# A norm after a matmul stage: the last block's squares summed by TensorE directly, its weight split and its products moved behind them

## The chip, the cores and the metric

The kernel runs on one core of one Trainium2 chip. The metric is the device time of one launch in microseconds (us). Engines are named as in the profile: PE is TensorE, DVE is VectorE, ACT is ScalarE, POOL is GpSimd, SP is SyncE (here it only issues weight loads).

## The reference

One sequence of 512 tokens with 1024 features goes through a conditioned block (gated mixer and convolution mixer, `w_out`, feed-forward of 2816), a final modulated norm, and then a second network: attention with two kinds of heads, a feed-forward, a pooling mixer and another feed-forward. What matters here is that each stage which ends in a product with a weight matrix is followed by a norm over the 1024 features of every token:

```python
def rmsnorm(x, g):
    xf = x.astype(jnp.float32)
    y = xf * lax.rsqrt(jnp.mean(xf * xf, axis=-1, keepdims=True) + EPS)
    return (y * g.astype(jnp.float32)).astype(x.dtype)
...
        x = x + gate1[:, None, :] * (y @ w_out[i])
        h2 = modulate(rmsnorm(x, norm2_g[i]), shift2, scale2)
```

In the first network the norm is taken of the renewed `x`. In the second it is taken of the stage's output `m`: `x` becomes `x + rmsnorm(m)`, and the norm of the new `x`, which opens the next stage, is derived from the sums of m*m, x*m and (gained m) squared.

## The kernel before

Features lie on the 128 partitions (8 chunks, `C`), tokens along the free axis (512). A weight matrix is read in blocks that give 128 output features: a block of 8 (or 11 for the down projections) tiles of 128x128. Each weight is split in a high and a low part so that three fast matmuls give fp32 accuracy: SP loads the raw block (`RAW`, 4 buffers), ACT rounds it to `WH` (L263, `split_hi`), DVE subtracts to get `WL` (L267, `split_lo`), 2 buffers each. PE computes a block with 3 matmuls per tile (L319 to L321) into one of two PSUM banks, and signals `mm`. ACT and DVE work in a written order of their own, one step per block: the split of the block two further on, and then the evacuation of the block that was just finished. `phase_splits` writes that order; at the last block of a stage the split step belongs to the second block of the next stage.

Six norms follow such a stage: `n2` after `w_out`, `nf` after `ffo0`, `r1` after `att_out`, `r2` after `ffo1`, `r3` after the pooling stage and `r4` after `ffo2`. The norm of each needs the sum of squares over all features of a token:

- In `n2` and `nf` DVE adds the gated bank to `X` (`dve_gated`, L513), ACT squares the chunk of `X` into `TMP` (`act_gated`, L522), DVE adds `TMP` to the running sum `ACC` (L518).
- In `r1`, `r2`, `r4` ACT (`act_m`) copies the bank to `M` with a gain (L528), squares it into `TMP` (L532 or L535) and, in `r1` and `r2`, squares the gained bank into `TMM` (L536); then DVE (`dve_m`) adds `TMP` to `ACC` (L555), multiplies `M` by `X` into `TXM` (L544) and adds `TMM` to `SMM` and `TXM` to `SXM` (`dve_cross`, L547 and L550). The pooling stage does the same in `pool_squares` (L1565, L1570, L1573) and `pool_sums` (L1965 to L1971).
- Then the chain of the norm: PE sums `ACC` over the partitions with four 1-column matmuls (`pe_sum`, L384, 8 records), DVE scales the mean (L408), POOL takes the power of -1/2 (L438), DVE lays it on a diagonal (L417), PE spreads it over all partitions (`pe_bcast`, L389, 2 records), and DVE starts on the normed chunks (L492, L586 or L569).

In `r1`, `r2`, `r3` PE sums `SXM` and `SMM` after the broadcast (`pe_sum_cross`). During `w_out` DVE also adds blocks of the conditioning matrix (`ada_step`, L1627), as many behind each block as `ADA_STEPS` says. In `r3` the splits of the first two blocks of `ffi2` run on DVE under the power and under the broadcast (`dve_renew`, `under_power` and `under_broadcast`).

Of the kernel before, what the change touches and what calls it, by code (L numbers as in the profile page):

```python
# [38 lines left out]
ADA_STEPS = [2, 2, 1, 1, 1, 1, 1, 1, 2, 2, 2, 2, 2, 0, 0, 0] + [2, 2, 2, 2, 1, 1, 1, 1]  # L39
# [34 lines left out]
def build_program(nc, xT, vec, ada_w, w_in, w_out, ffi, ffo, ln_rows, ws, bs, att_w, att_out, bf, pe, w1, w2,  # L74
                  pool_w, f2i, f2o, outT):
    ctx = ExitStack()
    with ctx:
# [160 lines left out]
        class Norm:  # L238

            def __init__(self, count, turn, at, n_acc_):  # L240
# [47 lines left out]
        def phase_splits(name, eng, step, evac):  # L288

            kc, nxt = kc_of(name), follow(name)  # L290
            uniform = nxt is not None and nxt[0] == kc
# [217 lines left out]
        def dve_gated(nj_, name, m, b, gate0):  # L509
# [5 lines left out]
                                           ALU.mult, ALU.add).then_inc(ev[b], 1)  # L515
            nc.vector.wait_ge(n_sq, nj_.sq + m[0] + 1)
# [410 lines left out]
        def _(pe_):  # L927
# [155 lines left out]
            pe_sum(nj["n2"])  # L1083
# [6 lines left out]
            pe_sum(nj["nf"])  # L1090
# [188 lines left out]
            pe_sum(nj["r1"])  # L1279
# [4 lines left out]
            pe_sum(nj["r2"])  # L1284
# [34 lines left out]
            pe_sum(nj["r3"])  # L1319
# [4 lines left out]
            pe_sum(nj["r4"])  # L1324
# [4 lines left out]
        def _(act):  # L1329
# [73 lines left out]
            def last_square(k):  # L1403
                if k == 1:
# [6 lines left out]
                         lambda g, t: act_gated(nj["n2"], "w_out", 4 * g + t, t % 2, 2 * g + t // 2))  # L1411
# [3 lines left out]
                         lambda g, t: act_gated(nj["nf"], "ffo0", 2 * g + t // 2, t // 2, g) if t % 2 else None)  # L1415
# [113 lines left out]
            def m_phase(name, r, norm_col, js=None):  # L1529
# [4 lines left out]
                else:  # L1534
                    phase_splits(name, act, act_step, lambda g, t: act_m(
                        nj[r], name, 4 * g + t, t % 2, N0[name] + 4 * g + t + 1,
                        VEC[:, bass.ds(COL["norm_g2"] + norm_col + 4 * g + t, 1)], js))
# [23 lines left out]
            def pool_squares(o):  # L1561
# [3 lines left out]
                act.activation(M[:, o, :], PS[b][:, :], ACT.Copy, scale=PG[:, o:o + 1])  # L1565
# [4 lines left out]
                act.activation(ACC if o == 0 else TMP[:, b, :], PS[b][:, :], ACT.Square, scale=vcol("pool_s", o))  # L1570
# [16 lines left out]
        def _(dve):  # L1587
# [471 lines left out]
```

## Time and profile before

| | us |
|---|---|
| median of 3 runs | 1854.68 (1853.14 to 1855.72) |
| the profiled execution | 1853.88 |
| its span, first to last instruction | 1852.1 |
| PE busy in the span | 1714.6 (93%) |
| DVE busy | 900.6 (49%) |
| ACT busy | 662.0 (36%) |
| POOL busy | 189.6 (10%) |

The profiled execution took 1.8 us more than its span, and 0.8 us less than the median. PE is busy for nearly all of the span, but "busy" holds time at the lower clock and time between a weight stage and the next. The page gives the mean granted TensorE clock as 0.959 of full speed.

### The profile page before, as it was taken

The page shows a single profiled execution, that of the slowest core. Times are in us where ns is not written, and L with a number is a line of the kernel's source. Part 1 is how long each engine was busy: PE and PEld are TensorE (multiplying, and loading weights), DVE is VectorE, ACT ScalarE, POOL GpSimd, SP SyncE. Part 2 cuts the span into 40 slices and gives each one's busy share as a digit, 9 for nine tenths or more (in the row PEclk, how much of TensorE's full clock was granted, in tenths as well). Part 3 has the DMA queues.
Part 4 walks back from the last instruction along what each step waited for, and adds up shares of the span by engine and source line. Part 5 has one row for each costly group of instructions (what it writes and reads, how often), then busy time and mean ns, then how long its engine had stood idle before and what let it go on. Part 6 is the DMA issues. An engine that isn't in the chain of part 4 may idle for free.

```text
span 1852.1 us, 21986 instructions
## 1 busy us (share of the span) xinstructions
PE 1714.6 (93%) x8095; PEld 1336.5 (72%) x8095; DVE 900.6 (49%) x1340; ACT 662.0 (36%) x949; POOL 189.6 (10%) x186
## 2 busy tenths in 40 slices
PE   2999889999999859999999899999998799999996
PEld 1657668888888637766667688888887588888884
DVE  6865674533322262355656644444334844444223
ACT  1324334444312241455555344443224433333221
POOL 4001119910000060000000000001100000000000
PEclk9999889999999969999999799999998799999998
DMA  8564144522322231111102122223221022223221
GB/s 284 197 204 146 65 163 170 181 91 102 108 94 93 68 62 66 58 46 35 35 24 69 47 101 92 100 91 117 93 76 54 32 99 97 96 96 114 93 77 46
DMA packets 49111, 179.73 MB, mean 97 GB/s; under 512 B 5984, under 2 KB 6656, under 8 KB 48928
## 3 DMA queue, kind: packets, MB, share of 16 engines
q1 hardware_dynamic: 44896, 166.75, 26.2%
q0 software_dynamic: 3008, 10.59, 2.1%
q10 hardware_dynamic: 1152, 1.66, 0.3%
q8 instruction: 34, 0.56, 0.1%
q14 instruction: 21, 0.17, 0.0%
HBM read 173.56 MB, written 2.10 MB: 95 GB/s over the span
## 4 chain that ended last, share of the span: by engine, by line
PE 66%; issue 22%; DVE 8%; ACT 2%; POOL 1%; DMA 1%; ACTq 1%; POOLq 0%; DVEq 0%; SPq 0%
PE bank L319 15%; PE bank L321 15%; PE bank L320 15%; PE bank L1138 3%; PE bank L1140 2%; PE bank L1139 2%; PE bank L1198 2%; PE bank L1242 2%; PE bank L1218 2%; DVE ada_acc L1598 1%; PE bank L389 1%; PE bank L1296 1%; PE bank L1123 1%; DVE tmp L492 1%; DMA raw<-in_ada_w 1%
## 5 line engine op out<-in xcount | busy, mean ns | idle before, releaser
L267 DVE TENSOR_TENSOR w_lo<-raw,w_hi 128x1024 fp32r<-128x1024 f32 (+1 forms) x236 | 319.1, 1352 | 684.9 <-ACT w_hi L263 684.8
L319 PE MATMUL bank<-h_hi,w_hi 128*128 128x512 f32 x1248 | 495.0, 397 | 6.9 <-DVE h_lo L485 3.5
L320 PE MATMUL bank<-h_lo,w_hi 128*128 128x512 f32 x1248 | 488.2, 391 | 0.0
L321 PE MATMUL bank<-h_hi,w_lo 128*128 128x512 f32 x1248 | 488.1, 391 | 0.0
L263 ACT ACTIVATE w_hi<-raw 128x1024 fp32r<-128x1024 f32 (+1 forms) x236 | 265.6, 1126 | 584.6 <-PE bank L321 516.0
L319 PEld LDWEIGHTS bank<-h_hi,w_hi 128*128 128x128 f32 x1248 | 235.6, 189 | 70.0 <-issue 11.0
L321 PEld LDWEIGHTS bank<-h_hi,w_lo 128*128 128x128 f32 x1248 | 235.7, 189 | 49.6
L320 PEld LDWEIGHTS bank<-h_lo,w_hi 128*128 128x128 f32 x1248 | 235.9, 189 | 48.2 <-issue 1.0
L319 PE MATMUL bank<-hid_hi,w_hi 128*128 128x512 f32 x528 | 209.4, 397 | 0.0
L321 PE MATMUL bank<-hid_hi,w_lo 128*128 128x512 f32 x528 | 209.2, 396 | 0.0
L320 PE MATMUL bank<-hid_lo,w_hi 128*128 128x512 f32 x528 | 209.1, 396 | 0.0
L438 POOL TENSOR_TENSOR stat<-stat,nhalf 128x4 f32<-128x4 f32 x10 | 11.1, 1111 | 1195.7 <-DVE stat L408 1195.7
L320 PEld LDWEIGHTS bank<-hid_lo,w_hi 128*128 128x128 f32 x528 | 99.4, 188 | 24.3
L321 PEld LDWEIGHTS bank<-hid_hi,w_lo 128*128 128x128 f32 x528 | 99.3, 188 | 24.4
L319 PEld LDWEIGHTS bank<-hid_hi,w_hi 128*128 128x128 f32 x528 | 99.3, 188 | 24.2
L384 PE MATMUL bank<-ones,tmp 128*128 128x1 f32 x80 | 15.9, 319 | 66.0 <-POOL tmp L464 43.8
L636 ACT ACTIVATE hid_hi<-tmp 128x512 f32 (+1 forms) x44 | 27.9, 635 | 119.8 <-DVE tmp L652 119.8
L384 PEld LDWEIGHTS bank<-ones,tmp 128*128 128x128 f32 x80 | 15.6, 286 | 70.2 <-issue 30.5
L1480 ACT ACTIVATE p_t<-bank 128x1024 f32<-128x1024 f32 (+4 forms) x52 | 37.9, 729 | 78.5 <-PE bank L1218 70.8
L1138 PE MATMUL bank<-h_hi,w_hi 128*128 128x512 f32 x128 | 59.1, 461 | 0.0
L1497 ACT ACTIVATE scores<-scores,att_stat 128x512 f32<-128x512 f32 (+3 forms) x96 | 52.8, 552 | 9.0 <-DVE att_stat L1873 8.9
L633 ACT ACTIVATE tmp<-tmp 128x512 f32<-128x512 f32 x44 | 27.8, 633 | 71.1 <-DVE tmp L645 71.1
(310 smaller groups left out, 1969.4 us busy)
## 6 DMA issues: line engine op xcount, KB each, us to landing
raw<-in_f2i SPq DMA_DIRECT2D x88, 512.0 KB, 3.2
raw<-in_ffi SPq DMA_DIRECT2D x44, 512.0 KB, 3.2
raw<-in_f2o SPq DMA_DIRECT2D x32, 704.0 KB, 4.0
ada_w<-in_ada_w SPq DMA_DIRECT2D x32, 512.0 KB, 4.1
raw<-in_att_w SPq DMA_DIRECT2D x24, 512.0 KB, 3.2
raw<-in_ffo SPq DMA_DIRECT2D x16, 704.0 KB, 4.0
raw<-in_ada_w SPq DMA_DIRECT2D x16, 512.0 KB, 4.7
raw<-in_w_in SPq DMA_DIRECT2D x16, 512.0 KB, 5.2
```

Of the source, the lines that this page charges most:

```text
L263: nc.scalar.activation(WH[par][:, 0:kc * P], RAW[s][:, 0:kc * P], ACT.Copy).then_inc(whi, 1)
L267: nc.vector.tensor_tensor(WL[par][:, 0:kc * P], RAW[s][:, 0:kc * P], WH[par][:, 0:kc * P].bitcast(F32), ALU.subtract).then_inc(wlo, 1)
L319: pe_.matmul(bank[:, :], w_h, hi[:, k0 + k, :], start=start and k == 0, stop=False)
L320: pe_.matmul(bank[:, :], w_h, lo[:, k0 + k, :], start=False, stop=False)
L321: last = pe_.matmul(bank[:, :], w_l, hi[:, k0 + k, :], start=False, stop=stop and k == kc - 1)
L1138: pe_.matmul(PS[t][:, :], w_h, hi[:, k, :], start=first, stop=False)
L1139: pe_.matmul(PS[t][:, :], w_h, lo[:, k, :], start=False, stop=False)
L1140: m = pe_.matmul(PS[t][:, :], w_l, hi[:, k, :], start=False, stop=last)
L1198: m = pe_.matmul(QB[:, half, 0:L], lhs, rhs, start=kind != "fox", stop=True)
L1218: m = pe_.transpose(TB[:, half, j * P:(j + 1) * P], sc[:, j * P:(j + 1) * P], IDN[:, :])
L1480: act.activation(dst[:, :, 0:L], TB[0:rows, :, 0:L], ACT.Copy).then_inc(a6["pt"], 1)
L1497: act.activation(sc, sc, ACT.Exp, scale=-1.0, bias=AST[:, 0, col:col + 1], accum_out=AST[:, 1, col:col + 1]).then_inc(a6["ex"], 1)
```

## The change

In all six norms the last block (chunk 7) is treated apart.

- ACT squares the bank first and signals `n_sq`; the copy to `M` and the gained square come behind. This new order holds for every block of `r1` to `r4`.
- DVE no longer adds the last chunk's squares to `ACC`. PE sums seven chunks from `ACC` and then the eighth from `TMP` (`pe_sum_last`: four matmuls, a wait on `n_sq`, four matmuls, accumulating in the same four columns).
- The split of the next stage's second block is held back: on ACT behind the last square, on DVE behind the diagonal (`n2`, `nf`, `r1`).
- In `r1`, `r2`, `r3` the last product is under the power and the last two sums are under the broadcast. The `ffi2` splits that were there go behind `r2`'s renewal, ahead of the pooling sums.
- In `w_out` the last ada step moves from behind block 7 to behind block 4, and the mean is issued ahead of the two small conditioning operations.

The diff, cut to its core:

```diff
-ADA_STEPS = [...] + [2, 2, 2, 2, 1, 1, 1, 1]
+ADA_STEPS = [...] + [2, 2, 2, 2, 2, 1, 1, 0]
...
+        def last_split(name, step):
+            kc, rnd = follow(name)
+            step(N0[name] + 4 * G[name] + 1, 1, 1, kc, rnd)
...
-                    elif nxt is not None:
+                    elif nxt is not None and not (hold and t == 3):
                         step(n + 2, t % 2, t - 2, nxt[0], nxt[1])
...
+        def pe_sum_last(nj_):
+            nc.tensor.wait_ge(n_acc, nj_.acc_end)
+            for i in range(TC):
+                nc.tensor.matmul(NS[:, i:i + 1], ACC[:, i * P:(i + 1) * P], ONE[:, 0:1], start=i == 0, stop=False,
+                                 skip_group_check=True)
+            nc.tensor.wait_ge(n_sq, nj_.sq + C)
+            for i in range(TC):
+                m = nc.tensor.matmul(NS[:, i:i + 1], TMP[:, 1, i * P:(i + 1) * P], ONE[:, 0:1], start=False,
+                                     stop=i == TC - 1, skip_group_check=True)
+            m.then_inc(n_used, 1)
...
         def act_m(nj_, name, m, b, done, gain, js):
             nc.scalar.wait_ge(mm, done)
-            nc.scalar.activation(M[:, bass.ds(m, 1), :], PS[b][:, :].rearrange("p (a s) -> p a s", a=1), ACT.Copy,
-                                 scale=gain)
             nc.scalar.wait_ge(n_acc, nj_.acc + m)
+            if js is not None:
+                nc.scalar.wait_ge(n_mms, 9 * js + m + 1)
+            nc.scalar.activation(TMP[:, b, :], PS[b][:, :], ACT.Square).then_inc(n_sq, 1)
+            into = nc.scalar.activation(M[:, bass.ds(m, 1), :], PS[b][:, :].rearrange("p (a s) -> p a s", a=1),
+                                        ACT.Copy, scale=gain)
             if js is None:
-                nc.scalar.activation(TMP[:, b, :], PS[b][:, :], ACT.Square).then_inc(ev[b], 1)
+                into.then_inc(ev[b], 1)
             else:
-                nc.scalar.wait_ge(n_mms, 9 * js + m + 1)
-                nc.scalar.activation(TMP[:, b, :], PS[b][:, :], ACT.Square)
                 nc.scalar.activation(TMM[:, b, :], PS[b][:, :], ACT.Square, scale=gain).then_inc(ev[b], 1)
...
         def dve_m(nj_, name, m, b, half, js):
-            nc.vector.wait_ge(ev[b], O0[name] // 2 + half + 1)
+            nc.vector.wait_ge(n_sq, nj_.sq + m + 1)
             nc.vector.wait_ge(n_acc, nj_.acc + m + 1)
             nc.vector.tensor_tensor(ACC, ACC, TMP[:, b, :], ALU.add).then_inc(n_acc, 1)
             if js is not None:
+                nc.vector.wait_ge(ev[b], O0[name] // 2 + half + 1)
+                dve_product(m, b)
                 dve_cross(m, b, js)
...
+            dve_mean(nj["n2"], D)
             dve.wait_ge(ada_sum, 5)
             dve.tensor_tensor(MOD[:, 24:40], PS[5][:, 24:40], VEC[...], ALU.add).then_inc(mod_ready, 1)
-            dve_mean(nj["n2"], D)
             dve.wait_ge(mod_ready, 6)
             gain(1, 32, "norm2").then_inc(mod_ready, 1)
             dve_diag(nj["n2"], D, mean=False)
+            last_split("w_out", dve_step)
...
             dve_diag(nj["nf"], D)
+            last_split("ffo0", dve_step)
...
-            dve_renew(nj["r1"], nj["q1"], 0, xs[1], g1_, dve_low(nj["q1"], xs[1], g1_))
+            def last_cross():
+                dve_cross(C - 1, 1, 0)
+                last_split("att_out", dve_step)
+            dve_renew(nj["r1"], nj["q1"], 0, xs[1], g1_, dve_low(nj["q1"], xs[1], g1_),
+                      under_power=lambda: last_product("att_out"), under_broadcast=last_cross)
...
-            dve_renew(nj["r2"], nj["q2"], 1, xs[2], None, None, spread=False)
+            dve_renew(nj["r2"], nj["q2"], 1, xs[2], None, None, spread=False,
+                      under_power=lambda: last_product("ffo1"), under_broadcast=lambda: dve_cross(C - 1, 1, 1))
+            split_lo(N0["ffi2"], 0, 0, C)
+            split_lo(N0["ffi2"] + 1, 1, 1, C)
...
-            for o in range(C):
+            for o in range(C - 1):
                 pool_sums(o)
...
-                      under_power=lambda: split_lo(N0["ffi2"], 0, 0, C),
-                      under_broadcast=lambda: split_lo(N0["ffi2"] + 1, 1, 1, C))
+                      under_power=lambda: pool_product(C - 1, 1), under_broadcast=lambda: pool_cross(C - 1, 1))
```

Where `pe_sum` stood for `n2`, `nf` and `r1` to `r4`, `pe_sum_last` stands now.

## Rows read from the trace of the kernel before

**Rows 1.** Page, part 4: the chain that ended last, shares by engine.

```profile
PE 66%; issue 22%; DVE 8%; ACT 2%; POOL 1%; DMA 1%; ACTq 1%; POOLq 0%; DVEq 0%; SPq 0%
```

**Rows 2.** Timeline about `n2`: start us, us, engine, line, op, out<-in [idle before <-releaser].

```profile
254.25 0.39 PE L321 MATMUL bank<-h_hi,w_lo 128*128 128x512 f32 x1
254.68 1.06 ACT L263 ACTIVATE w_hi<-raw 128x1024 fp32r<-128x1024 f32 x1 [3.32 <-PE bank L321]
255.76 1.23 DVE L267 TENSOR_TENSOR w_lo<-raw,w_hi 128x1024 fp32r<-128x1024 f32 x1 [2.49 <-ACT w_hi L263]
256.91 0.74 DVE L513 SCALAR_TENSOR_TENSOR x_res<-bank,mod,x_res 128x512 f32<-128x512 f32 x1
257.79 0.63 ACT L522 ACTIVATE tmp<-x_res 128x512 f32 x1 [2.05 <-DVE x_res L513]
258.45 0.69 DVE L518 TENSOR_TENSOR tmp<-tmp 128x512 f32<-128x512 f32 x1 [0.80 <-ACT tmp L522]
259.19 1.87 PE L384 MATMUL bank<-ones,tmp 128*128 128x1 f32 x8 [4.56 <-DVE tmp L518]
263.13 2.08 PE L389 MATMUL bank<-tmp,ones 128*128 128x512 f32 x2 [2.07 <-DVE tmp L417]
```

**Rows 3.** Timeline in `w_out`: a run of sixteen 1-column records, and an ada step.

```profile
247.24 1.84 PE L933 MATMUL bank<-ones,ada_acc 128*128 128x1 f32 x16
252.00 1.28 DVE L1627 SCALAR_TENSOR_TENSOR ada_acc<-ada_w,c_act,ada_acc 128x1024 f32<-128x1024 f32 x1
```

**Rows 4.** Timeline about `nf`: the last matmul of the stage and the sum.

```profile
640.03 0.39 PE L321 MATMUL bank<-hid_hi,w_lo 128*128 128x512 f32 x1
644.93 1.15 PE L384 MATMUL bank<-ones,tmp 128*128 128x1 f32 x8 [4.52 <-DVE tmp L518]
```

**Rows 5.** Timeline about `r1`.

```profile
1021.52 0.40 PE L1140 MATMUL bank<-ao_hi,w_lo 128*128 128x512 f32 x1
1023.49 0.59 ACT L535 ACTIVATE tmp<-bank 128x512 f32<-128x512 f32 x1
1025.53 1.86 PE L384 MATMUL bank<-ones,tmp 128*128 128x1 f32 x8 [3.60 <-DVE tmp L555]
1027.67 1.04 POOL L438 TENSOR_TENSOR stat<-stat,nhalf 128x4 f32<-128x4 f32 x1 [339.73 <-DVE stat L408]
1031.61 0.69 DVE L586 TENSOR_TENSOR tmp<-m_out,bank 128x512 f32<-128x512 f32 x1 [2.17 <-PE bank L389]
```

**Rows 6.** Timeline about `r2`.

```profile
1407.16 0.40 PE L321 MATMUL bank<-hid_hi,w_lo 128*128 128x512 f32 x1
1410.12 1.70 PE L384 MATMUL bank<-ones,tmp 128*128 128x1 f32 x8 [2.57 <-DVE tmp L555]
```

**Rows 7.** Timeline about `r3`: DVE's sixth sum, PE's sum, the split and the power.

```profile
1446.76 0.68 DVE L1965 TENSOR_TENSOR tmp<-tmp 128x512 f32<-128x512 f32 x1
...
1449.90 1.86 PE L384 MATMUL bank<-ones,tmp 128*128 128x1 f32 x8 [5.00 <-DVE tmp L1965]
...
1451.89 1.22 DVE L267 TENSOR_TENSOR w_lo<-raw,w_hi 128x1024 fp32r<-128x1024 f32 x1
1452.05 1.92 POOL L438 TENSOR_TENSOR stat<-stat,nhalf 128x4 f32<-128x4 f32 x1 [30.23 <-DVE stat L408]
```

**Rows 8.** Timeline about `r4`.

```profile
1831.48 0.40 PE L321 MATMUL bank<-hid_hi,w_lo 128*128 128x512 f32 x1
1833.87 1.05 PE L384 MATMUL bank<-ones,tmp 128*128 128x1 f32 x8 [1.99 <-DVE tmp L555]
```

**Rows 9.** Stretches (us, PE, PEld, DVE, ACT, POOL busy, granted clock, DMA share, GB/s).

```profile
254.65:256.62 1.97, 0.00 (x0) 0.00 (x0) 0.85 (x1) 1.06 (x1) 0.00 (x0) 1.00 0.00 0
640.42:645.74 5.32, 0.81 (x8) 0.81 (x8) 2.58 (x3) 1.69 (x2) 0.00 (x0) 1.00 0.29 99
1035.15:1048.51 13.36, 11.07 (x24) 7.29 (x25) 12.92 (x24) 4.34 (x6) 1.52 (x1) 0.50 0.00 0
```

**Rows 10.** Timeline: a broadcast at the higher clock.

```profile
1473.78 1.02 PE L404 MATMUL bank<-tmp,ones 128*128 128x512 f32 x2
```

More of the change, by code:

```diff
@@ L286, in kc_of, with is_last, phase_splits @@
             return KH if name.startswith("ffo") else C
-        def phase_splits(name, eng, step, evac):
+        def is_last(name, g, t):
+            return isinstance(g, int) and g == G[name] - 1 and t == 3
+        def last_split(name, step):
+            kc, rnd = follow(name)
+            step(N0[name] + 4 * G[name] + 1, 1, 1, kc, rnd)
+        def phase_splits(name, eng, step, evac, hold=False):
             kc, nxt = kc_of(name), follow(name)
-            uniform = nxt is not None and nxt[0] == kc
+            uniform = nxt is not None and nxt[0] == kc and not hold
             def body(g, last):
@@ L507, in dve_clear_acc, with dve_gated @@
             nc.vector.memset(ACC, 0.0).then_inc(n_acc, 1)
-        def dve_gated(nj_, name, m, b, gate0):
+        def dve_gated(nj_, name, m, b, gate0, last=False):
             cnt = O0[name] // 2
@@ L515, in dve_gated @@
                                            ALU.mult, ALU.add).then_inc(ev[b], 1)
+            if last:
+                return
             nc.vector.wait_ge(n_sq, nj_.sq + m[0] + 1)
@@ L1410, in _ @@
             phase_splits("w_out", act, act_step,
-                         lambda g, t: act_gated(nj["n2"], "w_out", 4 * g + t, t % 2, 2 * g + t // 2))
+                         lambda g, t: act_gated(nj["n2"], "w_out", 4 * g + t, t % 2, 2 * g + t // 2), hold=True)
+            last_split("w_out", act_step)
             act_parts(nj["n2"], C, shift=lambda k: MOD[:, 24 + k:25 + k])
@@ L1414, in _ @@
             phase_splits("ffo0", act, act_step,
-                         lambda g, t: act_gated(nj["nf"], "ffo0", 2 * g + t // 2, t // 2, g) if t % 2 else None)
+                         lambda g, t: act_gated(nj["nf"], "ffo0", 2 * g + t // 2, t // 2, g) if t % 2 else None, hold=True)
+            last_split("ffo0", act_step)
             act_squares(nj["q0"], C, lambda k: X[:, k, :], lambda k: act.wait_ge(xs[0], k + 1), sq_m)
@@ L1569, in pool_squares @@
                     act.wait_ge(n_acc, nj["r3"].acc + o)
-                act.activation(ACC if o == 0 else TMP[:, b, :], PS[b][:, :], ACT.Square, scale=vcol("pool_s", o))
+                act.activation(ACC if o == 0 else TMP[:, b, :], PS[b][:, :], ACT.Square,
+                               scale=vcol("pool_s", o)).then_inc(n_sq, 1)
+                act.activation(M[:, o, :], PS[b][:, :], ACT.Copy, scale=PG[:, o:o + 1])
                 if o >= 2:
@@ L1750, in _ @@
             for n in range(C):
-                split_lo(N0["w_out"] + n + 2, n % 2, (n + 2) % 4, C)
-                dve_gated(nj["n2"], "w_out", (n, N0["w_out"] + n + 1), n % 2, 16)
-                ada_step(16 + n)
+                if n < C - 1:
+                    split_lo(N0["w_out"] + n + 2, n % 2, (n + 2) % 4, C)
+                dve_gated(nj["n2"], "w_out", (n, N0["w_out"] + n + 1), n % 2, 16, last=n == C - 1)
+                if n < C - 1:
+                    ada_step(16 + n)
+            dve_mean(nj["n2"], D)
             dve.wait_ge(ada_sum, 5)
             dve.tensor_tensor(MOD[:, 24:40], PS[5][:, 24:40], VEC[:, COL["ada_b"] + 24:COL["ada_b"] + 40], ALU.add).then_inc(mod_ready, 1)
-            dve_mean(nj["n2"], D)
             dve.wait_ge(mod_ready, 6)
@@ L1773, in _ @@
             phase_splits("ffo0", dve, dve_step, lambda g, t: dve_gated(
-                nj["nf"], "ffo0", (2 * g + t // 2, N0["ffo0"] + 4 * g + t + 1), t // 2, 40) if t % 2 else None)
+                nj["nf"], "ffo0", (2 * g + t // 2, N0["ffo0"] + 4 * g + t + 1), t // 2, 40,
+                last=is_last("ffo0", g, t)) if t % 2 else None, hold=True)
             dve_diag(nj["nf"], D)
+            last_split("ffo0", dve_step)
             dve.wait_ge(n_rb, nj["nf"].turn)
@@ L1941, in m_phase, with last_product @@
                 if name.startswith("ffo"):
-                    phase_splits(name, dve, dve_step, lambda g, t: dve_m(nj[r], name, 2 * g + t // 2, t // 2, g, js) if t % 2 else None)
-                else:
-                    phase_splits(name, dve, dve_step, lambda g, t: dve_m(nj[r], name, 4 * g + t, t % 2, 2 * g + t // 2, js))
+                    phase_splits(name, dve, dve_step, lambda g, t: dve_m(nj[r], name, 2 * g + t // 2, t // 2, g, js)
+                                 if t % 2 and not is_last(name, g, t) else None, hold=True)
+                else:
+                    phase_splits(name, dve, dve_step, lambda g, t: dve_m(nj[r], name, 4 * g + t, t % 2, 2 * g + t // 2, js)
+                                 if not is_last(name, g, t) else None, hold=True)
+            def last_product(name):
+                dve.wait_ge(ev[1], O0[name] // 2 + 4)
+                dve_product(C - 1, 1)
             m_phase("att_out", "r1", 0)
             g1_ = lambda k: vcol("norm_g2", 16 + k)
-            dve_renew(nj["r1"], nj["q1"], 0, xs[1], g1_, dve_low(nj["q1"], xs[1], g1_))
+            def last_cross():
[3 more added lines that the diff above has]
+                      under_power=lambda: last_product("att_out"), under_broadcast=last_cross)
             phase_splits("ffi1", dve, dve_step, lambda g, t: dve_ffi_scaled("ffi1", ff[1], g, t, 1))
```

38 lines of the change are left out of this document (23 added, 15 removed).

## The prediction

> **What bounds the kernel now.** The chain of waits comes first: 66% of it is PE, 8% DVE, 2% ACT, 1% POOL [rows 1]. Inside a weight stage nothing but PE counts. DVE, ACT and POOL get onto the chain where a stage ends, so I then read the timeline about the six norms. The reader is to see in [rows 2] a file of single instructions: the last matmul ends at 254.64 (call such an end T), ACT splits, DVE splits, DVE gates, ACT squares, DVE adds, and only at 259.19, 4.55 us after T, does PE start the sum. Whatever leaves this file leaves the time. Third come the stretches, for the clock.
>
> **From the last matmul to the sum.** Six cases.
>
> n2: the splits put the gating at 256.91; without them it starts as soon as `mm` is seen, T + 0.05 (ACT's own start behind T is 0.04). From gating to square is 0.88, from square to its end 0.63, and PE starts 0.05 behind its input [rows 2]: T + 1.61 in place of T + 4.55, 2.95 less. Against it stands the moved ada step: 1.28 [rows 3], or 1.38 as the second of two, earlier on DVE. DVE idled 2.49 before its split [rows 2], that is from 253.27, so it is now free at about 254.65, just T. I take off 0.1; up to 0.5 if it slips. PE's seven-chunk matmuls run meanwhile, in the 1.6 us it would idle.
>
> nf: T is 640.42 and the sum started at 644.93 [rows 4], 4.51 behind. The same new file gives 1.61: 2.9 less. No ada work here.
>
> r1: T is 1021.92, the sum came 3.61 later [rows 5], behind a split (1.06), a copy, the square, the gained square (DVE waited for the bank's release, which only that gives) and the add. Now the square is first: 0.04 + 0.59 + 0.05 = 0.68. PE's own four matmuls come first, though: sixteen such records took 1.84 at the full clock, and began 0.17 before the matmul ahead of them had ended [rows 3], so eight are over at T + 0.75. I take T + 0.8: 2.8 less. If the eight cost a full 1.05 [rows 8] behind T and then a wait, it is 0.3 to 0.5 less of a gain in r1, r2 and r4 each.
>
> r2: T is 1407.56, sum at + 2.56 [rows 6]; no split stood there. 1.75 less. r4: T is 1831.88, sum at + 1.99 [rows 8]: 1.2 less.
>
> r3: here DVE is the laggard, four operations at 0.60 each per chunk, and the end of the seventh add at 1449.86 gates PE. Two things change. DVE can begin chunk 1's add when the square is there and not at the bank's release, 0.6 earlier, and being saturated keeps that; and PE needs only the sixth add, which ended at 1447.44 [rows 7], now 1446.85. The eighth square is done before that (ACT was ahead of DVE), so PE has two sums in a row: 16 records. At the full clock 1.84 to 2.1, mean at 1449.0; at half clock twice 1.86, mean at 1450.6. Before, the mean was at 1451.81. I take 1449.6, since the clock was still full until 1447.87: 2.2 less, with ends 1.2 and 2.8.
>
> **The sum itself.** It took 1.87, 1.15, 1.86, 1.70, 1.86, 1.05 [rows 2, 4 to 8]: the longer ones at a granted clock of 0.5, the level of 1.2 GHz, the shorter at 2.4 GHz. How long PE stood before the clock fell varies: 1.97 us behind T in n2, 5.32 in nf [rows 9], and 2.7, 2.8, 3.0, 5.1 in r1, r2, r3, r4, by further rows of this view. New sums end at T + 1.8 to 2.7, before nearly all of these, so I price them all at 1.1: 0.75 less in n2 and r1, 0.6 in r2, nothing in nf and r4.
>
> **From mean to broadcast.** In r1, r2 and r3 the product M*X (two SBUF inputs, 0.69) now runs beside POOL's power. The row to read is r3's: the split (two SBUF inputs, to 1453.11) began just before the power, which took 1.92 where r1's took 1.04 [rows 5, 7]; it ended 0.86 behind the split. A product from mean + 0.08 to mean + 0.77 therefore puts the power's end at mean + 1.64, not + 1.25: 0.4 lost in r1 and r2. In r3 the split goes, and 1.92 becomes 1.4: 0.5 won. If the product does not hold POOL, each is 0.4 better; if it holds it for its whole length, 0.3 worse.
>
> The Trainium skill (SBUF — State Buffer, Who interferes with whom) says that a DVE instruction with two SBUF inputs contends with a GpSimd instruction that reads SBUF, and that the one that comes second waits out the whole of the first. It speaks against putting products under the power. Read to the letter it makes the power 0.55 late (the overlap), not 0.4, 0.45 us more over the three norms; the trace agrees in kind, with 0.9 lost on an overlap of 1.06.
>
> Under the broadcast DVE idled 2.17 [rows 5]. One split (1.15 to the next start) fits in n2 and nf; two sums (1.2) fit in r2 and r3; in r1 sums and split make 2.35, so r1 loses 0.1 to 0.2. The `ffi2` splits moved into the pooling stage fall where DVE waited over 4 us for the first pooled chunk: nothing. SP's load behind a held-back split leaves some 4 us later for a block due four blocks (22 us) on: nothing.
>
> **The broadcast.** It took 2.08 at half clock [rows 2], in all six; at the full clock the same shape took 1.02 [rows 10]. New broadcasts start at T + 4.8 (n2, nf), T + 4.3 (r1, r2), T + 3.9 (r4). By the fall times above, r4's would be at the full clock (1.05 less), half of nf's (0.5), the others at half. I take 1.5, with ends 0 and 4.
>
> **Sum.** n2 2.95 - 0.1 + 0.75 = 3.6; nf 2.9; r1 2.8 + 0.75 - 0.4 - 0.1 = 3.05; r2 1.75 + 0.6 - 0.4 = 1.95; r3 2.2 + 0.5 = 2.7; r4 1.2; broadcasts 1.5. Together 16.9. Each shift reaches the end, because what follows hangs on the broadcast: chunk by chunk on DVE, then PE. Against the profiled execution's 1853.88 that is 1837.0; the median of the runs lies 0.8 above it, 1837.8. I say 1837.5.
>
> **The rivals.**
>
> A, fewer gains (0.13): PE's first four matmuls land on the path (1.2 over three norms), r3's sums run at half clock (1), no broadcast gets the full clock (1.5), DVE slips in n2 (0.4), and PE restarts at half clock for longer. Gain 9 to 13, time 1841.5 to 1846. For it: the clock fell 1.97 us after T once. Against: the sums fill the gap.
>
> B, the clock holds (0.14): the 2 to 5 us for which PE stood before the sum are gone or filled, only the 2.1 between sum and broadcast stay [rows 2], and the clock no longer falls before the broadcast. Then four more broadcasts save up to 1 each, less in r1, where DVE's own 2.35 covers it, and part of the restart is faster. Gain 20 to 23, time 1831.5 to 1834.5. For it: nf and r4 kept the clock 5 us. Against: four of six did not.
>
> C, no change (0.02): something else released PE after each norm anyway, weights or conditioning. After n2 PE waited for its own conditioning sums, but these sit behind the broadcast and move with it. Time 1854.
>
> D, slower (0.02): the clock's restart. After r1 PE worked 13.36 us at half clock, though busy for 11.07 of them [rows 9]. A matmul start takes 0.43 there against 0.23. If each restart stayed at half clock longer, a microsecond more costs 0.47; to eat 16.9 it takes 36 us in all, over 7 us at each of five restarts. From there the kernel is slower; at 10 us each it would be 1861. Nothing in the rows ties the restart to the pause's length.
>
> **How the numbers follow.** The forecast has 0.69 (gains of 13 to 20). The range 1833 to 1843 takes in the forecast's bounds, most of B and the near end of A. About 0.2% (3.7 us) is what a measurement can tell from no change. Faster by more than that: 0.95; within: 0.03; slower: 0.02.
>
> **What would show it.** In the new profile: the square (or the gating) starts within 0.1 us of the last matmul's end; L384's successor has two sets of 8 records, the second ending about T + 1.8 (r1, r2, r4) and T + 2.7 (n2, nf), each near 1.1; the power in r1, r2, r3 takes 1.4; the split in n2, nf, r1 stands under the broadcast; r3's mean comes some 4.7 us after the last window matmul and not 6.9. It is wrong if the power takes 1.0 or 1.9, if the first set of sums starts well behind T, or if PE waits in `w_out` for the bank of block 5.

## The result, and the profile after

The changed kernel takes **1836.7 us** (median of 4 runs, 1834.38 to 1839.55). The kernel before took 1853.91 in the same rounds (1851.29 to 1855.72). The ratio is 0.9912, 95% interval 0.9897 to 0.9928: faster, and 0.8 us from the 1837.5 predicted. Run again unedited (a0_after below) it was 1837.55, ratio 0.9926 [0.9911, 0.9941]. One of e3_early's four runs took 1985.21 at a mean granted clock of 0.83 and is left out of its numbers below.

The profiled execution of the changed kernel took 1838.76, with a span of 1837.0. First the chain of waits (page, part 4), which answers to [rows 1]: ACT's 2% has become 1%, PE has one per cent more, of a shorter span.

```profile
PE 67%; issue 21%; DVE 8%; ACT 1%; POOL 1%; DMA 1%; ACTq 1%; POOLq 0%; DVEq 0%; SPq 0%
```

Now the timeline about `n2` in the changed kernel, which answers to [rows 2]. Its T (end of the stage's last matmul) is 256.69.

```profile
256.30 0.39 PE L330 MATMUL bank<-h_hi,w_lo 128*128 128x512 f32 x1
256.52 0.94 PE L400 MATMUL bank<-ones,tmp 128*128 128x1 f32 x8
256.72 0.75 DVE L534 SCALAR_TENSOR_TENSOR x_res<-bank,mod,x_res 128x512 f32<-128x512 f32 x1 [0.33 <-PE bank L330]
257.51 0.63 ACT L545 ACTIVATE tmp<-x_res 128x512 f32<-128x512 f32 x1 [3.03 <-DVE x_res L534]
...
258.19 1.05 PE L404 MATMUL bank<-ones,tmp 128*128 128x1 f32 x8 [0.72 <-ACT tmp L545]
...
259.52 1.01 POOL L459 TENSOR_TENSOR stat<-stat,nhalf 128x4 f32<-128x4 f32 x1 [53.65 <-DVE stat L429]
260.56 0.69 DVE L438 TENSOR_TENSOR tmp<-ident,stat 128x512 f32<-128x512 f32 x1 [0.83 <-POOL stat L459]
261.17 1.22 DVE L267 TENSOR_TENSOR w_lo<-raw,w_hi 128x1024 fp32r<-128x1024 f32 x1
261.31 2.08 PE L410 MATMUL bank<-tmp,ones 128*128 128x512 f32 x2 [2.06 <-DVE tmp L438]
...
263.50 1.41 DVE L513 SCALAR_TENSOR_TENSOR tmp<-x_res,gs,bank 128x512 f32<-128x512 f32 x2 [1.11 <-PE bank L410]
```

The reader is to see the file of five become a file of three. The gating starts 0.03 us after T, the square behind it. The first set of sums (L400) lies under the gating, and the second starts 1.50 after T where the only sum started 4.55 after it. The split that stood ahead of the gating (L267) now starts at 261.17 and ends 1.00 before the broadcast does. Only the broadcast is as it was: 2.08, the lower clock.

The same view about `r1` (T 1019.15), which answers to [rows 5]:

```profile
1019.00 0.95 PE L400 MATMUL bank<-ones,tmp 128*128 128x1 f32 x8
1019.20 0.60 ACT L554 ACTIVATE tmp<-bank 128x512 f32<-128x512 f32 x1 [2.84 <-PE bank L1169]
1019.69 0.68 ACT L555 ACTIVATE m_out<-bank,vec_sb 128x512 f32<-128x512 f32 x1
1019.85 1.05 PE L404 MATMUL bank<-ones,tmp 128*128 128x1 f32 x8
...
1020.94 0.16 DVE L429 TENSOR_SCALAR stat<-bank 128x4 f32<-128x4 f32 x1 [2.56 <-PE bank L404]
1021.01 0.68 DVE L568 TENSOR_TENSOR h_scratch<-m_out,x_res 128x512 f32<-128x512 f32 x1
1021.18 1.42 POOL L459 TENSOR_TENSOR stat<-stat,nhalf 128x4 f32<-128x4 f32 x1 [336.12 <-DVE stat L429]
...
1023.38 2.07 PE L410 MATMUL bank<-tmp,ones 128*128 128x512 f32 x2 [2.48 <-DVE tmp L438]
1023.84 0.68 DVE L577 TENSOR_TENSOR h_scratch<-h_scratch 128x512 f32<-128x512 f32 x1
1024.44 1.22 DVE L267 TENSOR_TENSOR w_lo<-raw,w_hi 128x1024 fp32r<-128x1024 f32 x1
...
1025.58 0.68 DVE L615 TENSOR_TENSOR tmp<-m_out,bank 128x512 f32<-128x512 f32 x1
```

The second set starts 0.70 after T, without a wait between the sets. The power took 1.42 with the product (L568) beside it, 1.04 without [rows 5]. L615 (the first DVE instruction that reads the broadcast) has no idle time ahead of it now: DVE's own work, not the broadcast, is what ends last there, and L615 starts 0.13 after the broadcast ended at 1025.45, where it started 0.03 after it before.

About `r3` (its last window matmul ends at 1435.12), which answers to [rows 7]:

```profile
1436.36 0.68 DVE L2018 TENSOR_TENSOR tmp<-tmp 128x512 f32<-128x512 f32 x1
...
1437.10 1.05 PE L400 MATMUL bank<-ones,tmp 128*128 128x1 f32 x8 [1.99 <-DVE tmp L2018]
...
1438.01 1.75 PE L404 MATMUL bank<-ones,tmp 128*128 128x1 f32 x8
...
1439.80 0.16 DVE L429 TENSOR_SCALAR stat<-bank 128x4 f32<-128x4 f32 x1 [0.95 <-PE bank L404]
1439.88 0.68 DVE L2024 TENSOR_TENSOR h_scratch<-m_out,x_res 128x512 f32<-128x512 f32 x1
1440.04 1.39 POOL L459 TENSOR_TENSOR stat<-stat,nhalf 128x4 f32<-128x4 f32 x1 [28.05 <-DVE stat L429]
```

PE waits 1.99 for the add, not 5.00. The clock falls in the second set (1.75, not 1.05). In the other profiles of kernels with this order it fell earlier still, as a0_after below shows, so that this one is the favourable case. About `nf` (T 640.56) and `r4` (T 1818.99), which answer to [rows 4, 8]:

```profile
642.07 1.21 PE L404 MATMUL bank<-ones,tmp 128*128 128x1 f32 x8 [0.72 <-ACT tmp L545]
...
1819.67 1.05 PE L404 MATMUL bank<-ones,tmp 128*128 128x1 f32 x8
1820.76 0.16 DVE L429 TENSOR_SCALAR stat<-bank 128x4 f32<-128x4 f32 x1 [13.44 <-PE bank L404]
...
1822.79 1.12 PE L410 MATMUL bank<-tmp,ones 128*128 128x512 f32 x2 [2.07 <-DVE tmp L438]
```

r4's broadcast alone found the full clock. One measure serves for all that follows: from T to the first DVE instruction that reads the broadcast.

| us from T | n2 | nf | r1 | r2 | r3 | r4 | sum |
|---|---|---|---|---|---|---|---|
| before | 10.67 | 9.88 | 9.69 | 8.45 | 11.95 | 7.22 | 57.86 |
| after | 6.81 | 6.93 | 6.43 | 6.29 | 9.20 | 5.04 | 40.70 |
| gain | 3.86 | 2.95 | 3.26 | 2.16 | 2.75 | 2.18 | 17.16 |
| predicted | 3.6 | 2.9 + 0.5 | 3.05 | 1.95 | 2.7 | 1.2 + 1.05 | 16.9 |

The spans differ by only 15.1, though. The distances between the T's tell where the other 2 went: start to n2 2.05 longer; then shorter by 1.91 (to nf), 2.91 (r1), 4.91 (r2), 2.11 (r3), 3.10 (r4) and 2.21 (end). From nf on, each is the gain of its norm to within 0.4; r1's has 1.7 on top, as the first two blocks of `ffi1`, the renewed phase behind it (it starts on the chunks as DVE renews them), ran less long at the lower clock (18.7 us from their third matmul to their last before, 17.1 now). That is not shown to be the change's work: in a0_after they took 18.6. The two early ones fall short because of the clock, in places that the change doesn't touch. By stretches (columns as in [rows 9]), the changed kernel and then the kernel before:

```profile
210.00:220.00 10.00, 8.72 (x30) 6.64 (x30) 5.92 (x11) 3.45 (x5) 0.00 (x0) 0.83 0.00 0
...
504.00:514.00 10.00, 10.00 (x59) 8.87 (x57) 3.63 (x4) 3.24 (x3) 0.00 (x0) 0.96 0.37 135
514.00:524.00 10.00, 10.00 (x35) 8.09 (x35) 1.89 (x5) 0.63 (x1) 0.00 (x0) 0.70 0.22 74
```

```profile
210.00:220.00 10.00, 8.45 (x36) 6.51 (x37) 6.83 (x12) 3.90 (x6) 0.00 (x0) 1.00 0.01 2
...
510.00:520.00 10.00, 10.00 (x55) 8.72 (x54) 3.74 (x6) 2.01 (x2) 0.00 (x0) 0.83 0.43 144
```

A mean of 0.83 over 10 us is 3.4 us at half clock, 1.7 us of work lost; so 1.7 are lost in the first stretch. In the second the changed kernel has 0.8 + 6.0 us at half and the kernel before 3.4, which makes 1.7 again. So the profiled pair understates the norms' own 17.16. That the medians differ by 17.2 is no second proof of that number: the ratio's interval stands for 13 to 19 us, and a0_after's ratio for 13.7.

### The profile page after: what moved, and what is told of

The parts are those of the page before. It is cut to its first block, busy times and chain, and to the rows that moved or that the text cites. A ratio compares the mean times of both kernels' runs of the same rounds, so it can differ in the third digit from the quotient of the medians.

```text
span 1837.0 us, 22013 instructions
## 1 busy us (share of the span) xinstructions
PE 1716.6 (93%) x8143; PEld 1339.8 (73%) x8143; DVE 898.1 (49%) x1334; ACT 661.1 (36%) x949; POOL 189.4 (10%) x186
## 4 chain that ended last, share of the span: by engine, by line
PE 67%; issue 21%; DVE 8%; ACT 1%; POOL 1%; DMA 1%; ACTq 1%; POOLq 0%; DVEq 0%; SPq 0%
PE bank L328 16%; PE bank L329 15%; PE bank L330 15%; PE bank L1167 3%; PE bank L1169 2%; PE bank L1168 2%; PE bank L1227 2%; PE bank L1271 2%; PE bank L1247 2%; DVE ada_acc L1631 1%; PE bank L1325 1%; PE bank L1152 1%; DVE tmp L513 1%; DMA raw<-in_ada_w 1%; PE bank L410 1%
## 5 line engine op out<-in xcount | busy, mean ns | idle before, releaser
L267 DVE TENSOR_TENSOR w_lo<-raw,w_hi 128x1024 fp32r<-128x1024 f32 (+1 forms) x236 | 322.5, 1367 | 679.1 <-ACT w_hi L263 678.8
L329 PE MATMUL bank<-h_lo,w_hi 128*128 128x512 f32 x1248 | 488.2, 391 | 0.0
L330 PE MATMUL bank<-h_hi,w_lo 128*128 128x512 f32 x1248 | 488.1, 391 | 0.0
L1168 PE MATMUL bank<-h_lo,w_hi 128*128 128x512 f32 x128 | 50.4, 394 | 0.0
L1169 PE MATMUL bank<-h_hi,w_lo 128*128 128x512 f32 x128 | 50.3, 393 | 0.0
```

Source lines behind the costliest of these rows:

```text
L267: nc.vector.tensor_tensor(WL[par][:, 0:kc * P], RAW[s][:, 0:kc * P], WH[par][:, 0:kc * P].bitcast(F32), ALU.subtract).then_inc(wlo, 1)
L329: pe_.matmul(bank[:, :], w_h, lo[:, k0 + k, :], start=False, stop=False)
L330: last = pe_.matmul(bank[:, :], w_l, hi[:, k0 + k, :], start=False, stop=stop and k == kc - 1)
L1168: pe_.matmul(PS[t][:, :], w_h, lo[:, k, :], start=False, stop=False)
L1169: m = pe_.matmul(PS[t][:, :], w_l, hi[:, k, :], start=False, stop=last)
```

## Experiments

The sum below is that of the table (40.70 in the changed kernel's first profile, 41.60 in its second). A ratio is always to the kernel before in the same rounds. One kernel's executions differ by 1.6 to 7 us; two profiles of one kernel differ mostly in where the clock falls. Where differences are small the traces decide, and where a trace differs in the clock alone it is one throw of several.

**The split ahead of the last evacuation again** (n2, nf, r1), all else kept.

```diff
         def last_split(name, step):
-            kc, rnd = follow(name)
-            step(N0[name] + 4 * G[name] + 1, 1, 1, kc, rnd)
+            return
...
-                    elif nxt is not None and not (hold and t == 3):
+                    elif nxt is not None:
```

> The changed kernel with one part undone: the split of the next stage's second block stands ahead of the last evacuation again, on ACT and DVE, in n2, nf and r1. Theory (the instructions ahead of the square are the price, one by one): in n2 and nf the gating starts 2.2 us later and all behind it with it; in r1 only ACT's split, 1.06, is ahead of the square, less 0.15 that the split cost under the broadcast; together 2.2 + 2.2 + 0.9 = 5.3 us, and up to 1.5 more if the sums fall to the lower clock: 1842 to 1843.5 against 1836.7. r2, r3, r4 as they are. Rival (the gain is mostly the sum on TensorE and the clock that it keeps up): under 2 us, 1838.

Measured: 1846.46, ratio 0.9955 [0.9939, 0.9972]; sum 49.46 (n2 9.92, nf 9.87, r1 7.33), 8.8 more, where the time is 9.8 longer. More than the 5.3 to 6.8 expected, but the three norms of the edit account for 6.95 of it; the rest lies in r3 (10.06) and r4 (5.99), which the edit doesn't touch and which a0_after has nearly so (9.82, 5.98). The timeline about n2 in this kernel (T 255.17) shows why:

```profile
255.27 1.06 ACT L263 ACTIVATE w_hi<-raw 128x1024 fp32r<-128x1024 f32 x1 [2.29 <-PE bank L329]
256.36 1.23 DVE L267 TENSOR_TENSOR w_lo<-raw,w_hi 128x1024 fp32r<-128x1024 f32 x1 [1.45 <-ACT w_hi L263]
257.50 0.75 DVE L533 SCALAR_TENSOR_TENSOR x_res<-bank,mod,x_res 128x512 f32<-128x512 f32 x1
...
258.96 1.87 PE L403 MATMUL bank<-ones,tmp 128*128 128x1 f32 x8 [3.00 <-ACT tmp L544]
```

The second set starts 3.79 after T, 2.29 later than in the changed kernel, which is the split's worth. Then it takes 1.87 and not 1.05: PE waited 3.00, not 0.72, and the clock had fallen. The split costs 2.3 by itself and 0.7 to 0.8 through the clock, in n2 and nf each.

**The last square added by DVE again**, one set of sums.

```diff
+        def last_add(nj_):
+            nc.vector.wait_ge(n_sq, nj_.sq + C)
+            nc.vector.wait_ge(n_acc, nj_.acc + C)
+            nc.vector.tensor_tensor(ACC, ACC, TMP[:, 1, :], ALU.add).then_inc(n_acc, 1)
...
-            pe_sum_last(nj["n2"])
+            pe_sum(nj["n2"])
```

> The changed kernel with one part undone: the last chunk's squares are added to the running sum by DVE and PE sums once (8 records), the splits and products stay where the change put them. Theory: n2, nf, r1, r2, r4 each lose one DVE add, 0.7 us, from the end of the square to PE's sum; in r3 the add waits behind the chunk before (2.4 us) but PE has only 8 records in place of 16, so 1.2 to 1.8; together 3.5 + 1.5 = 5.0 us: 1841.7. The mean comes at T + 2.5 in r1, r2, r4 (T the end of the last matmul) where it came at T + 1.8. Rival (PE's own first set of four matmuls costs as much as DVE's add): no difference in r1, r2, r4, 1838 to 1839 in all.

Measured: 1841.33, ratio 0.9938 [0.9922, 0.9955]; sum 46.78. As expected. In n2, nf, r1 and r2 the mean comes 3.32, 3.32, 2.50 and 2.50 after T, 0.72 later than with the direct sum in n2 and r2 (2.59, 1.78): the add's 0.69 and one more hand-over. In r3 it is 1.6 (6.30 for 4.68), since there DVE's own file is the laggard; against the 5.30 of a0_after, where both sets of sums ran at the lower clock for most of their time, it is 1.0.

**Both undone together.** Left are the square as the first operation, r3's order, the product under the power, and the `ffi2` splits moved away from r3's power (1.92 before, 1.38 here). The edit is the two above.

> The changed kernel with two of its parts undone together: the split before the last evacuation is back in n2, nf and r1, and the last square is added by VectorE again, with one set of sums on TensorE. Left of the change are the square as the first operation on the last block (r1, r2, r4), r3's order (add at the square, not at the bank's release), and the product under the power. Theory, the parts add up: of the changed kernel's 40.7 us from last matmul to the first normalized VectorE operation over the six norms, undoing the split alone gave 3.1 (n2), 2.9 (nf), 0.9 (r1) back, undoing the direct sum alone 0.7, 0.6, 0.7, 0.7, 1.6 and 0.7 to 1.7. Both: n2 10.6, nf 10.5, r1 8.0, r2 7.0, r3 10.8, r4 6.0 to 6.8, together 53 to 54 where the kernel before has 57.9; the time 4 to 5 us under the kernel before, 1849 to 1850. Rival 1, the parts hide one another (VectorE's split and its add run beside the same wait, so undoing both costs less than the sum): n2 and nf stay under 10.2, together under 52.5, 1847 to 1848.5. Rival 2, square first and product under the power are worth nothing by themselves: within 1.5 us of the kernel before.

Measured: 1850.01, ratio 0.9985 [0.9976, 0.9994]; sum 54.62, against 53 to 54 expected. From the ratios (times 1853.9): all 16.3 us (13.3 to 19.1), without the split's move 8.3, without the direct sum 11.5, with neither 2.8. So the split is worth 8.0, the direct sum 4.8 and the rest 2.8, together 15.6; each ratio is uncertain by 2 to 3 us to either side, so these are rough. By the sums of the traces the split is worth 7.9 to 8.8, the direct sum 5.2 to 6.1 and the rest 3.2, according to which profile of the changed kernel is taken (41.60 or 40.70), together 16.3 of 16.3 or 18.1 of 17.2. Within 1 us the parts add up, and none hides another. n2 took 10.64 here, as before the change: there these two parts are everything.

**The product ahead of the mean**, off the power. DVE stands idle before the mean in r1 (2.56 in the rows above); a semaphore on the copy to M lets it take the product then.

```diff
+                into.then_inc(n_cp, 1)
...
-            dve_mean(r, D)
             under_power()
+            dve_mean(r, D)
```

> The changed kernel with the last product M*X of r1, r2, r3 issued ahead of the mean, as soon as the copy to M is there, and no longer beside POOL's power. Theory (DVE's product with two SBUF inputs holds up POOL's power): the power takes 1.0 in place of 1.4 in all three; in r1 and r2 the mean itself comes up to 0.1 later because the product ends just then; from mean to broadcast 2.45 becomes 2.05; together 1.0 us less: 1835.7, too little for the clock on the wall, so the rows decide. Rival (the power is longer for another reason, such as its own start): it stays at 1.4.

Measured: 1834.04 (three runs, 1832.6 to 1837.05), ratio 0.9892 [0.9872, 0.9912]; sum 40.92. Timeline about r1 in this kernel (T 1017.28):

```profile
1018.52 0.69 DVE L570 TENSOR_TENSOR h_scratch<-m_out,x_res 128x512 f32<-128x512 f32 x1 [2.02 <-ACT m_out L556]
...
1019.13 0.15 DVE L430 TENSOR_SCALAR stat<-bank 128x4 f32<-128x4 f32 x1
1019.37 1.04 POOL L460 TENSOR_TENSOR stat<-stat,nhalf 128x4 f32<-128x4 f32 x1 [336.21 <-DVE stat L430]
```

The power takes 1.04, 1.01 and 1.01 in r1, r2 and r3, where it took 1.42, 1.39 and 1.39. The mean pays 0.07. So the product was what held POOL, and 0.38 was the price. The time's own interval does not tell this kernel from the changed one; the rows do.

**The moved ada step put back** behind block 7 of `w_out`.

```diff
-ADA_STEPS = ... + [2, 2, 2, 2, 2, 1, 1, 0]
+ADA_STEPS = ... + [2, 2, 2, 2, 1, 1, 1, 1]
...
-                if n < C - 1:
-                    ada_step(16 + n)
+                ada_step(16 + n)
```

> The changed kernel with the last ada step behind block 7 of w_out again, but behind the gating and ahead of the mean. Theory (DVE waits there for square and sum anyway: 1.8 us between gating and mean): nothing on the path, n2's mean at T + 2.6 as now, and DVE reaches the last gating with 1.3 us to spare in place of 0.33; 1836.7 within 0.5. Rival (the step had to move): the mean comes up to 1.3 us later, 1838.

Measured: 1836.24, ratio 0.9905 [0.9888, 0.9921]; in n2 the mean comes 2.59 after T and the first normalized operation 6.82, to 0.01 as in the changed kernel. The step lies behind the gating, in time in which DVE waits for the sum. Its move neither cost nor brought anything.

**The changed kernel unedited**, in the rounds of the three that follow.

> The changed kernel itself, unedited, on the same chip and in the same rounds as the three with filled pauses, to compare them with. All theories: 1836 to 1838, the clock at half for four or five of the six broadcasts, at 2.08 us each.

Measured: 1837.55, ratio 0.9926 [0.9911, 0.9941]. In this profile nf's broadcast took 1.58 and r4's 2.08, and r3's two sets of sums 1.57 and 1.84, its mean 5.30 after T and not 4.68; the sum is 41.60. Two more kernels have the six norms of the changed kernel, e4_ada_back above and h1_spread below. Their sums are 42.46 and 42.27, with all six broadcasts at 2.07 or 2.08 and r3's mean at 5.42 and 5.45. So of four profiles the first is the luckiest, and the norms' gain is 15.4 to 17.2 us, 16.1 on the mean. Where the clock falls isn't fixed: r4's fell 2.5 us after T here and 4.8 in the first profile, with the same work ahead of it.

**Does PE's work between sum and broadcast keep the clock?** Rival B put to the test: seven matmuls of ones (128 columns) behind the second set of sums in all six norms.

```diff
+        def idle_turns(count):
+            for _ in range(count):
+                nc.tensor.matmul(PS[4][:, 0:P], ONE[:, :], ONE[:, :], start=True, stop=True)
...
             m.then_inc(n_used, 1)
+            idle_turns(7)
```

> The changed kernel with seven 128-column fp32 matmuls of ones on PE (0.26 us each at the full clock, 1.8 in all, into a bank nobody reads) behind each norm's last sum, in the 2.1 to 2.5 us for which PE waits for the broadcast's diagonal. Theory (the pause lets the clock fall, as rival B of the prediction has it): the clock stays at full, all six broadcasts take 1.1 in place of 2.08; n2 and nf gain 1.0, r2 1.0 and its sixteen 1-column sums behind it 1.6, r3 1.0, r1 nothing since DVE has 2.35 us of work under the broadcast; 4 to 6 us in all: 1831 to 1833. Rival 1 (the clock falls anyway): no gain. Rival 2 (the filling runs past the diagonal): each broadcast starts up to 1.5 us later, 1840 or more.

Measured: 1838.26, ratio 0.9924 [0.991, 0.9939]: no time won, against 1831 to 1833 expected. The sum is 40.16, 1.4 less than a0_after's. Timeline about n2 in this kernel (T 254.77):

```profile
256.27 1.08 PE L408 MATMUL bank<-ones,tmp 128*128 128x1 f32 x8 [0.72 <-ACT tmp L550]
257.22 3.34 PE L398 MATMUL bank<-ones 128*128 128x128 f32 x14
...
260.35 1.14 PE L415 MATMUL bank<-tmp,ones 128*128 128x512 f32 x2
```

The clock fell at the end of the second set, before the first filling. So the fillings ran at half (3.34 us; where the clock held, in r3 of the next kernel, 1.81) and put off the broadcast: it starts 2.96 after the mean in place of 2.03. It then takes 1.14, and the two cancel. nf and r3 are alike (2.80 and 2.95 after the mean). In r1, r2 and r4 the broadcast took 1.12, as in the three filled kernels below, where the four profiles of the same norms without fillings (the first, a0_after, e4 and h1) have 2.07 or 2.08 (r4 once 1.12). r1 gained nothing by it, since DVE's own file is what ends last there (rival B had said "less in r1"), r2 gained 0.95 and r4 0.94.

These gains are lost again behind n2, outside the sum. From n2's T to nf's T this kernel needs 385.51 us, a0_after 383.95. Its rows there:

```profile
271.90 3.51 DVE L513 SCALAR_TENSOR_TENSOR h_lo<-tmp,mod,h_hi 128x512 fp32r<-128x512 f32 x2
...
272.48 2.37 POOL L896 TENSOR_TENSOR m_out<-m_out 128x1024 f32<-128x1024 f32 x1
...
275.46 0.51 PE L328 MATMUL bank<-h_hi,w_hi 128*128 128x512 f32 x1 [1.80 <-DVE h_lo L513]
```

And the same two instructions in a0_after:

```profile
269.93 1.62 DVE L508 SCALAR_TENSOR_TENSOR h_lo<-tmp,mod,h_hi 128x512 fp32r<-128x512 f32 x2
...
272.04 2.41 POOL L891 TENSOR_TENSOR m_out<-m_out 128x1024 f32<-128x1024 f32 x1
```

DVE's last two chunks take 3.51 and not 1.62, and PE waits 1.80 for them. In a0_after they end at 271.55, 0.49 ahead of POOL's sum for the conditioning; here that sum starts 1.4 us earlier after T (17.71, not 19.15), ahead of the last chunk, and DVE ends 0.56 behind it. POOL starts earlier because PE's sixteen conditioning sums behind the broadcast, which release it, took 1.84 at the full clock and not 3.41. All four filled kernels have this wait of 1.80 or 1.81, and none of the unfilled ones does. That POOL's sum is what holds DVE is read from the order of these rows; no run moves it away.

**Fillings in r3 and in the renewed phases too**: seven ahead of r3's sums, seven ahead of `ffi1` and `ffi2` and four in each of their steps 1 to 3.

```diff
+            idle_turns(7)
...
+                if 0 < step <= LAG:
+                    idle_turns(4)
...
+            idle_turns(7)
             pe_sum_last(nj["r3"])
```

> As f1_fill, and such matmuls also in r3 ahead of the first sum (7), between the sums behind the broadcast and the first matmul of ffi1 and ffi2 (7), and in the first three chunk steps there (4 each), where PE waits for DVE's chunks. Theory: the clock stays full through the restart too; the first two blocks of ffi1 and ffi2, 17 to 18.8 us from the first to the last matmul in the traces so far, come down to 16.5 to 17, r3's two sums take 2.0 in place of 2.8 to 3.6: 1.5 to 3.5 us beyond f1_fill: 1828 to 1831. Rival (DVE's chunks bound the restart and not PE): no gain beyond f1_fill, or a loss where a filling matmul stands ahead of a chunk that is ready.

Measured: 1833.24, ratio 0.9901 [0.9886, 0.9917]; sum 37.99, mean clock 0.976 against 0.965. Short of the 1828 to 1831 expected. Timeline about r3 in this kernel (T 1432.13):

```profile
1434.11 1.05 PE L407 MATMUL bank<-ones,tmp 128*128 128x1 f32 x8 [0.42 <-DVE tmp L2027]
...
1435.03 1.03 PE L411 MATMUL bank<-ones,tmp 128*128 128x1 f32 x8
...
1435.92 1.81 PE L401 MATMUL bank<-ones 128*128 128x128 f32 x14
...
1438.50 1.12 PE L418 MATMUL bank<-tmp,ones 128*128 128x512 f32 x2 [0.77 <-DVE tmp L446]
```

With PE at work before the sums, both sets and the broadcast are at the full clock: 7.53 from T, not 9.20 or 9.82. The first two blocks of `ffi1` and `ffi2` took 16.1 and 15.4 us from their third matmul to their last; the changed kernel's two profiles have 17.1 and 17.5, 18.6 and 18.5.

**Fillings and the early product together.**

> As f2_fill_all, with the product ahead of the mean as in e3_early. Theory: the two are independent, since one shortens POOL's power and the other the broadcast: 1.0 us beyond f2_fill_all, 1827 to 1830. Rival: the pause between sum and broadcast is then 0.4 shorter in r1, r2, r3 (2.06), the 1.8 us of filling still fit, so nothing is lost; if they do not fit, the broadcast comes later and the gain of e3_early is gone.

Measured: 1832.0, ratio 0.9901 [0.9887, 0.9915], all five runs (1829.14 to 1834.93) below all five of a0_after (1836.41 to 1840.55), but above the 1827 to 1830 expected. The profile is of the fastest of its runs: sum 36.28, clock 0.982. The ratio is f2's, so what the early product adds doesn't show in the time.

**The conditioning sums spread.** Between `ffi0` and `ffo0` the changed kernel runs 32 one-column records in a row, and in both its profiles the clock falls there.

```diff
-            for j in range(2):
-                ada_sums(ADA_N - 2 + j, PS[5], late_used, C * (j + 1))
...
+            for t in range(4):   # the last four blocks of ffi0, one sum after each step
+                block(..., spread)
```

> A place that the change does not touch. Between ffi0 and ffo0 the changed kernel runs 32 one-column records in a row (16 sums for the conditioning), 510.48 to 514.90, PE busy throughout, and the granted clock falls in them: 1.00 in 510 to 512, 0.78 in 512 to 514, 0.50 until 520. Here each of the 16 sums stands behind a step of three 512-column matmuls in the last four blocks of ffi0. Theory (one-column records leave the clock to fall, although PE counts as busy): the fall goes. The kernel before had 0.83 in its 510 to 520 (3.4 us at half, 1.7 lost), the changed one about 6.8 at half (3.4 lost); so 1.7 to 3.4 us less, ratio to the kernel before 0.9895 to 0.990 where the changed kernel had 0.9912 and 0.9926, and no stretch of 490 to 530 under 0.98. Rival 1 (the fall comes from the change of phase, transfers or weights, not from the one-column records): the clock falls there all the same, ratio 0.991 to 0.9925. Rival 2 (a one-column sum between long matmuls costs more than in a row, as it breaks the row of 512-column streams): the clock holds but the four blocks grow by more than the 4.0 us that the row took; nothing gained.

> The best version so far (fillings in the pauses, and the product ahead of the mean) with the same spread of the 16 conditioning sums over the last four blocks of ffi0. Theory: the same 1.7 to 3.4 us come off its 0.9901 of the kernel before, so 0.9883 to 0.9892, 1829 to 1831 us, granted clock 0.984 or more. Rival 1: no change, 0.990 to 0.9905. Rival 2: sums cost more when spread, 0.991.

Measured: h1_spread 1836.39, ratio 0.991 [0.9893, 0.9926]; h2_spread_best **1830.3** (1828.74 to 1831.62), ratio 0.9875 [0.9859, 0.9892], the fastest of all. h1_spread misses its expected 0.9895 to 0.990, h2_spread_best is a little better than its 0.9883 to 0.9892. Stretches of h1_spread, where the sums now stand (x57) and where the clock had fallen:

```profile
490.00:500.00 10.00, 10.00 (x57) 8.56 (x55) 1.92 (x2) 1.96 (x3) 0.00 (x0) 1.00 0.47 144
...
510.00:520.00 10.00, 10.00 (x45) 8.10 (x44) 3.76 (x7) 2.02 (x2) 0.00 (x0) 1.00 0.43 144
```

The fall is absent in both, and in h1_spread n2's T to nf's T is 381.08 us where it was 383.87 (the norm's own part equal to 0.01). But the clock also held over the row of 32 in the profiles of e2_dve_add, g1_square_only and f3_both, 3 of the 11 that have the row, and e2's distance is 381.11 though its norm is 0.73 longer. So two profiles without a fall don't show that the spreading removes it, and the size stays open too: h2's span (1827.3) is no shorter than f3's (1827.4), and its distance (384.12, with the 1.8 us of waiting behind n2) is f3's (384.28). The ratios, 0.9901 and 0.9875, speak for a gain, but their intervals overlap, and h1's 0.991 is the changed kernel's.

## Why the prediction was right

The forecast (0.69) is what happened, and by its mechanism: the norms gained 15.4 to 17.2 us where 16.9 was the sum. That the first profile's 17.16 is so near to 16.9 is partly luck: n2, r1 and r2 gained a little more than their terms, the broadcasts less, and r3 hit its term in this profile alone. By its own steps:

- **The file from T to the sum.** n2: predicted start T + 1.61, measured 1.50; the square follows the gating's start by 0.79, not 0.88. nf 1.51. r1, r2, r4: predicted 0.8, measured 0.70, 0.69, 0.68: the first set is over before the square is, so the dearer end (0.3 to 0.5 each) didn't come, nor rival A with it.
- **The sums** took 1.05 in four norms (1.1 predicted), 1.21 in nf and 1.75 in r3's second. Together with the earlier starts, n2, r1 and r2 gained 0.2 to 0.3 each more than their terms.
- **r3.** Mean predicted 4.7 after T, measured 4.68. The exact hit is luck: 5.30, 5.42 and 5.45 in the three other profiles of these norms, so that the norm gained 2.0 to 2.1 and not 2.75. The bounds (1449.0 and 1450.6, that is 4.1 and 5.7 after T) were real: f2, with PE kept at work, measured 3.97.
- **The power.** Predicted 1.4 with the product beside it, measured 1.42, 1.39, 1.39; e3 took the product away and had 1.01 to 1.04. In r1 the power ended 0.91 after the product, in r3's row before 0.86 after the split: this is the reading that the estimate rested on. The Trainium skill (SBUF — State Buffer, Who interferes with whom) has the second of the two wait out the first, which by the letter is the overlap: here 1021.18 to 1021.69, 0.51, where 0.38 was lost. The runs agree in kind, and the estimate from r3's row was nearer.
- **Under the broadcast.** n2, nf: hidden. r1: predicted 0.1 to 0.2 over, measured 0.1 (0.13 after the broadcast, 0.03 before the change).
- **The ada step.** 0.1 was taken off for its move; nothing came of it, and e4 shows that there was nothing to move it for.
- **The broadcasts**, the one term that is not as written: 1.5 predicted. In the first profile r4's came (2.08 to 1.12) and nf's half did not (2.07), 1.0 in all; in a0_after nf had 0.5 and r4 nothing; in e4 and h1 neither had anything. That is 0.4 on the mean, inside the stated ends of 0 and 4. The step that failed is the reading of fall times: it took how long the clock had held behind T in one profile (5.1 us in r4, 5.3 in nf) as belonging to the norm, and the same norm's clock fell at 2.5 in one execution and at 4.8 in another.

Rival B (1831.5 to 1834.5) did not come by itself. Its mechanism is real (with PE at work in the pause, r1, r2 and r4 had the full clock in all four filled profiles), but its premise, that shorter pauses are enough, fell: the pause from sum to broadcast was still 2.06, and in n2 and r3 the clock fell before or in it. Rival D's restart did not grow: behind r1 it was 1.7 us shorter in the first profile and as long as before in a0_after.

## What to carry to other kernels

At the end of a stage, list single instructions from the last matmul to the next matmul, and move what nobody in that file needs (here a split for a block two ahead) under the engine that works alone later: it was about half of the gain. An addition whose result goes into a matmul against ones can be left to the accumulation in the bank; its price is a second set of sums, and that lies in PE's idle time except in r3, where the two sets run one behind the other. Price each shortened wait at both clocks, take the clock from several profiles and not from one, and ask what an earlier finish releases: here it put a sum on POOL in front of DVE's last chunk.

## What was not expected

- **The clock fell while PE was busy.** PE counts as fully busy in 504 to 514, yet within the 4.42 us of 32 one-column records the granted clock went from 1.00 to 0.50, and the 512-column records behind it took 0.63, not 0.39, for 5 us. It fell in or right behind this row in 8 of 11 profiles and held in 3, so it is likely there and not certain; what decides was not found.
- **A filled pause paid only where the filling began ahead of the fall.** The same seven matmuls took 3.34 us behind it (n2 in f1_fill) and 1.81 ahead of it (r3 in f2_fill_all), and a gain in one place was lost to POOL's sum in the next.
